# A two-block transformer on one core: attention and its projections in one stage

## The reference

```python
def diff_attention(q, k, v, q_gain, k_gain, ...):
    q = rms_norm(q, q_gain)
    k = rms_norm(k, k_gain)
    ...
    s = jnp.einsum('bqhmd,bkhmd->bhmqk', q_blk, k).astype(jnp.float32) * DIFF_HD ** -0.5
    s = jnp.where(dist >= 0, s + bias[None, :, None], NEG_INF)
    p = jax.nn.softmax(s, axis=-1)
    attn = (p[:, :, 0] - lam * p[:, :, 1]).astype(v.dtype)
```

## Time and profile before

| what | us |
|---|---|
| three runs | 3668.67, 3671.29 (median), 3679.3 |
| profiled execution, its own time | 3667.99 |
| its span | 3666.2 |
| differential projection and attention | about 252 to 418 |
| sliding-window projection and attention | about 440 to 567 |
| three dilated projections and attentions | about 2590 to 3015 |

### The profile page before, as it was taken

One profiled execution on the slowest core, in us unless ns is written; L12 is line 12 of the kernel. 1 busy time (PEld: TensorE's weight loads), 2 busy tenths in 40 slices (PEclk: granted clock), 3 DMA queues, 4 the chain that ended last, 5 costly groups with the idle time before them and its releaser, 6 DMA issues. The chain is left out here.

```text
span 3666.2 us, 46186 instructions
## 1 busy us (share of the span) xinstructions
PE 3096.4 (84%) x18486; PEld 2461.0 (67%) x18486; DVE 2236.7 (61%) x2018; ACT 1594.5 (43%) x1705; POOL 252.8 (7%) x149
## 2 busy tenths in 40 slices
PE   8747668995899999999999918788778777979999
PEld 6625446774688888887888716687546665767777
DVE  5246553343699989999999934465555454346543
ACT  5433232221577777777777704222233331233322
POOL 0000000002011111111111000242000000000000
PEclk9878679996799999999999958899879777989999
DMA  8211011221699999999999841000202111223322
GB/s 295 94 53 52 12 35 58 92 104 64 252 371 377 372 375 371 379 373 374 372 378 373 336 150 54 25 4 14 75 23 64 41 46 43 93 61 92 92 81 80
DMA packets 216481, 604.82 MB, mean 165 GB/s; under 512 B 11426, under 2 KB 108706, under 8 KB 182788
## 3 DMA queue, kind: packets, MB, share of 16 engines
q1 hardware_dynamic: 206960, 568.52, 42.6%
q0 software_dynamic: 9216, 33.56, 2.4%
q10 hardware_dynamic: 148, 0.53, 0.0%
HBM read 581.57 MB, written 21.01 MB: 164 GB/s over the span
## 5 line engine op out<-in xcount | busy, mean ns | idle before, releaser
L1661 DVE TENSOR_TENSOR weight_ring_part<-weight_ring,weight_ring_part 128x2048 fp32r<-128x2048 f32 x384 | 861.6, 2284 | 95.2 <-ACT weight_ring_part L1602 95.1
L1602 ACT ACTIVATE weight_ring_part<-weight_ring 128x2048 fp32r<-128x2048 f32 x384 | 721.2, 1915 | 249.2 <-PE ps L192 136.6
L192 PE MATMUL ps<-weight_ring_part 128*128 128x512 f32 (+1 forms) x1328 | 527.0, 397 | 0.0
L287 DVE TENSOR_TENSOR weight_ring_part<-weight_ring,weight_ring_part 128x2048 fp32r<-128x2048 f32 x135 | 308.1, 2283 | 353.7 <-ACT weight_ring_part L284 351.6
L284 ACT ACTIVATE weight_ring_part<-weight_ring 128x2048 fp32r<-128x2048 f32 x135 | 257.0, 1904 | 401.0 <-PE ps L192 178.5
L190 PE MATMUL ps<-weight_ring_part,gathered_hi 128*128 128x512 f32 x1024 | 409.6, 400 | 1.7 <-DVE gathered_lo L1670 1.7
L192 PE MATMUL ps<-weight_ring_part,gathered_hi 128*128 128x512 f32 x1024 | 406.0, 396 | 0.0
L191 PE MATMUL ps<-weight_ring_part,gathered_lo 128*128 128x512 f32 x1024 | 405.9, 396 | 0.0
L190 PE MATMUL ps<-h1T_hi,weight_ring_part 128*128 128x512 f32 (+1 forms) x776 | 317.7, 409 | 55.0 <-PEq L339 30.2
L191 PE MATMUL ps<-h1T_hi,weight_ring_part 128*128 128x512 f32 (+1 forms) x776 | 306.9, 395 | 0.0
L192 PEld LDWEIGHTS ps<-weight_ring_part 128*128 128x128 f32 (+1 forms) x1328 | 252.7, 190 | 57.2 <-issue 1.0
(11 more groups left out here) (451 smaller groups left out, 4881.9 us busy)
## 6 DMA issues: line engine op xcount, KB each, us to landing
weight_ring<-in_w SPq DMA_DIRECT2D x190, 2048.0 KB, 8.5
weight_ring<-in_w_in SPq DMA_DIRECT2D x58, 1024.0 KB, 5.3
weight_ring<-in_w_ada SPq DMA_DIRECT2D x24, 1024.0 KB, 5.2
weight_ring<-in_w_ffn_up SPq DMA_DIRECT2D x44, 512.0 KB, 5.0
weight_ring<-in_w_ffn_down SPq DMA_DIRECT2D x11, 1024.0 KB, 4.9
chosen_rows<-y_rows SPq DMA_DIRECT2D x4, 2048.0 KB, 13.4
weight_ring<-in_w_branch SPq DMA_DIRECT2D x6, 1024.0 KB, 5.0
x_tok<-in_x SPq DMA_DIRECT2D x2, 2048.0 KB, 9.3
```

The costliest lines, as they stand in the source:

```text
L192: return nc.tensor.matmul(out, x[0], y[1], start=False, stop=stop)
L287: self.nc.vector.tensor_tensor(lo, full, hi, ALU.subtract).then_inc(self.split, 1)
L1602: nc.scalar.activation(hi_half(h), full_half(h), ACT.Copy).then_inc(w_rounded, 1)
L1661: nc.vector.tensor_tensor(lo_half(h), full_half(h), hi_half(h), ALU.subtract).then_inc(w_split, 1)
```

## The change

The projection and the attention of each kind become one stage, streamed. All engines walk one list, plan, of products ("prod"), per-token sums ("sums"), key scalings ("spread") and attention beats ("beat"). plan_of makes it: the products of the first batch (v, then two chunks of q and two of k), then one product of the next batch, the sums, and the rest of the next batch's products with the batch's units laid between them. Batches of the differential attention have 8 and 8 units, those of the sliding window 4 and 4 (with all seven products ahead of them), those of the dilated groups 8, 8, 2, 2, 2, 2 in one stage of 36 products and 24 units. A unit of the last two groups is now one pair of heads with all four residues, not one residue with all heads. Products alternate between two banks, and v comes first.

The norms change: the squares of a 128-token tile are the stationary operand of a matmul with two columns of head_sum, so that a batch gets 32 sums a partition; root and reciprocal are taken on those. For q the factor is applied where the bias is added, one instruction per segment (head and map, or head and residue). For k it is written out to 512 columns, transposed by a matmul with the identity, and multiplied into the key tile; both gains and the scale go into the copy of k. The biases of the dilated groups are loaded by pairs of heads in the background.

```diff
@@ -348,11 +347,16 @@
...
-        for j in range(6):
-            ring.add_pair(wide(w_in, 512 * j), DK, 512, by_rows=(j == 4))
+        for j in range(2):
+            ring.add_pair(wide(w_in, 512 * j), DK, 512, by_rows=False)
+        ring.add_pair(wide(w_in, 2048), DK, 512, by_rows=True)
+        for half in range(2):
+            for j in (2, 3):
+                ring.add(wide(w_in, 512 * j)[:, :, 256 * half:256 * half + 256], DK, 256)
         w_kv = a["w_kv"].rearrange("(k p) n -> p k n", p=P)
         ring.add(w_kv[:, :, 0:256], DK, 256)
         ring.add(w_kv[:, :, 256:384], DK, P)
...
@@ -890,7 +897,350 @@
...
                             read_out(i - 3)
 
+        def plan_of(n_elements, batches, units_of, ahead=()):
+
+
+            plan, beat = [("prod", e) for e in range(batches[0]["ends"])], 0
+            for b, batch in enumerate(batches):
+                stop = batches[b + 1]["ends"] if b + 1 < len(batches) else n_elements
+                products = list(range(batch["ends"], stop))
+                beats = list(range(beat, beat + units_of[b]))
+                beat += units_of[b]
+                spreads = [("spread", (b, j)) for j in range(len(batch["keys"]))]
+                head, rest = products[:1], products[1:]
+                plan += [("prod", e) for e in head] + [("sums", b)]
+                slots = max(len(rest), 1)
+                for n in range(slots):
+                    if n < len(rest):
+                        plan.append(("prod", rest[n]))
+                    if n == 0:
+                        plan += spreads
+                    share = beats[len(beats) * n // slots:len(beats) * (n + 1) // slots]
+                    plan += [("beat", i) for i in share]
+            return plan + [("beat", beat + n) for n in range(3)]
...
+            def rounded_after(e):
+                x = elements[e]
+                if x["kind"] == "v" and not x["ends"]:
+                    return first_unit + x["unit"]
+                pair = e + 1 < len(elements) and x["ends"] and elements[e + 1]["kind"] == "v"
+                return first_unit + x["unit"] + (2 if pair else 1)
+
...
+                @block.tensor
+                def _(pe):
...
+                    def prod(e):
+                        x = elements[e]
+                        need = (0, 1) if x["kind"] == "v" else (0,)
+                        for u in (x["unit"] - (len(need) - 1) + n for n in need):
+                            if u not in w:
+                                w[u] = ring.take(pe)
+                        if e >= 2:
+                            copied(pe, e - 2)
...
+                        if x["ends"]:
+                            pe.wait_ge(group_ready, e + 1)
+                            for _ in range(x["ends"]):
+                                nc.tensor.nop().then_inc(ring.used, 1)
...
+                    def sums(b):
+                        pe.wait_ge(squared, squared_at[batches[b]["elements"][-1]])
...
+                        for j, e in enumerate(batches[b]["elements"]):
+                            for t in range(TT):
+                                at = 8 * j + 2 * t
+                                last = nc.tensor.matmul(ps[:, 2, at:at + 2], sq[:, slot_of_square(e), elements[e]["tokens"](t)], head_sum[:, 0:P:HD],
+                                                        start=True, stop=True)
+                        last.then_inc(summed, 1)
+
+                    def spread(b, j):
+                        pe.wait_ge(factors_ready, b + 1)
+                        pe.wait_ge(keys_scaled, spread_at[b, j])
+                        wide = sq[:, slot_of_square(batches[b]["keys"][j]), :]
+                        for t in range(TT):
+                            last = nc.tensor.matmul(ps[:, 2, P * t:P * t + P], wide[:, P * t:P * t + P], ident, start=True, stop=True)
+                        last.then_inc(spread_ready, 1)
...
+                    def beat(i):
+                        if 2 <= i < N + 2:
+                            u = units[i - 2]
+                            pe.wait_ge(probs_ready, i - 1)
+                            if i >= 3:
+                                pe.wait_ge(turned_read, i - 2)
+                            for j, c in enumerate(u["turns"]):
+                                last = nc.tensor.transpose(t_bank[:, P * j:P * j + P], s_buf[:, (i - 2) % 3, c:c + P], ident)
+                            last.then_inc(turned, 1)
...
+                            for c, n, lhsT, rhs, _, _ in u["scores"]:
+                                last = nc.tensor.matmul(scores[:, c:c + n], lhsT, rhs, start=True, stop=True)
+                            last.then_inc(scores_ready, 1)
...
+                @block.scalar
+                def _(act):
+                    def prod(e):
+                        x = elements[e]
+                        ring.ahead("act", act, first_unit + x["unit"])
+                        act.wait_ge(group_ready, e + 1)
...
+                        if x["kind"] == "k":
+                            nc.scalar.activation(x["dst"], ps[:, e % 2, :], ACT.Identity, scale=x["gain"], bias=0.0).then_inc(bank_free[e % 2], 1)
+                        else:
+                            nc.scalar.activation(x["dst"], ps[:, e % 2, :], ACT.Copy).then_inc(bank_free[e % 2], 1)
+                        ring.ahead("act", act, min(rounded_after(e), first_unit + n_units))
...
+                    def sums(b):
...
+                        nc.scalar.activation(root(b)[:, 0:m], ps[:, 2, 0:m], ACT.Sqrt, scale=1.0 / HD, bias=col("eps")).then_inc(rooted, 1)
...
+                @block.vector
+                def _(dve):
...
+                    def sums(b):
...
+                        nc.vector.reciprocal(factor(b)[:, 0:m], root(b)[:, 0:m])
+                        dve.drain()
+                        for e in batches[b]["keys"]:
+                            at = 8 * batches[b]["elements"].index(e)
+                            nc.vector.tensor_copy(sq[:, slot_of_square(e), :].rearrange("p (n d) -> p n d", n=8),
+                                                  factor(b)[:, at:at + 8].unsqueeze(2).to_broadcast([P, 8, HD]))
+                        dve.drain().then_inc(factors_ready, 1)
+
+                    def spread(b, j):
+                        e = batches[b]["keys"][j]
+                        copied(dve, e)
+                        dve.wait_ge(spread_ready, spread_at[b, j] + 1)
+                        dst = elements[e]["dst"]
+                        nc.vector.tensor_tensor(dst, dst, ps[:, 2, :], ALU.mult).then_inc(keys_scaled, 1)
...
+                            s_row = s_buf[:, i % 3, :]
+                            for c, m, _, _, q_at, bias in u["scores"]:
+                                last = nc.vector.scalar_tensor_tensor(s_row[:, c:c + m], scores[:, c:c + m], factor(u["batch"])[:, q_at:q_at + 1],
+                                                                      bias, ALU.mult, ALU.add)
+                            last.then_inc(scores_read, 1)
...
@@ -980,21 +1331,28 @@
-        project(hT, [[("norm", gains[:, 0:1], dqT[:, m, :], True) for m in range(BC)],
-                     [("norm", col("diff_knorm"), dkT[:, m, :], True) for m in range(BC)],
-                     token_groups(dv)], scratch4)
+        natural = lambda t: slice(P * t, P * t + P)
+        elements = [dict(kind="v", unit=1, ends=(2 if t == 3 else 0), dst=dv[:, t, :], tok=lambda h, k, t=t: h[:, k, P * t:P * t + P])
+                    for t in range(TT)]
+        for pair in range(2):
+            for kind, buf in (("q", dqT), ("k", dkT)):
+                for part in range(2):
+                    elements.append(dict(kind=kind, unit=2 + 2 * pair + (kind == "k"), part=part, ends=part, dst=buf[:, 2 * pair + part, :],
+                                         gain=gains[:, 0:1], tokens=natural))
+        batches = [dict(ends=8 + 4 * pair, elements=[4 + 4 * pair + n for n in range(4)], keys=[6 + 4 * pair, 7 + 4 * pair]) for pair in range(2)]
         units = []
...
-        attention(units, stats, s_buf, p_turned)
...
+        streamed(hT, elements, batches, units, plan_of(12, batches, [8, 8]), scratch4, factors, stats, s_buf, p_turned)
...
@@ -1028,36 +1386,31 @@
...
+        elements = [dict(kind="k", unit=0, part=g, ends=g, dst=skT[:, g, :], gain=gains[:, 1:2], tokens=natural) for g in range(2)]
+        elements.append(dict(kind="vT", unit=1, part=0, ends=1, dst=svT, turned=sv))
+        elements += [dict(kind="q", unit=2 + m // 2, part=m % 2, ends=m % 2, dst=sqT[:, m, :], tokens=natural) for m in range(BC)]
+        batches = [dict(ends=5, elements=[0, 1, 3, 4], keys=[0, 1], after_v=True), dict(ends=7, elements=[5, 6], keys=[], slot0=2)]
...
+        plan = plan_of(7, batches, [4, 4])
+        plan.insert(4, ("turn_v", 2))
+        streamed(hT, elements, batches, units, plan, scratch_x, factors, stats, s_buf, p_turned)
...
-            with stage("alibi_loaded") as (block, alibi_loaded):
...
```

(12 more changed lines are left out.)

382 lines of the change are left out of this document (295 added, 87 removed).

## The result

The changed kernel takes 3750.8 us (median of 4, 3750.6 to 3752.8) against 3673.5 for the kernel before in the same sessions: ratio 1.0209 (95% interval 1.0196 to 1.0223). Slower, as forecast, but by 77 us instead of the 30 of the forecast's sum, and above its range (3655 to 3722).

The account below looks back on a forecast made before the run. Projections were taken as bound by TensorE, attentions by the round of scores, softmax and transposes over three engines. Differential +28, sliding window +3 and dilated -1 make +30 on 3667.99, giving 3698 us; range 3655 to 3722.

Parts of the forecast that it names:

- the differential stage: Differential projection and attention streamed as one stage: +28 us, bounds +14 and +36.
- the open stretch ahead of unit 8: Differential attention: the second batch's chain of sums, root, reciprocal, copies and spreads stands open between units 7 and 8, 9 us.
- the sliding window: Sliding-window stage, all seven products ahead of unit 0, nothing overlapping: +3 us, bounds -4 to +9.
- rival A: Shared stages keep TensorE at 2.4 GHz, so units between products cost their floor: -12 us, 3656; chance 0.17.
- 415 to 435: Dilated stage: a length of 415 to 435 us in the profile after would show the forecast right.
- Three projections of 76.2 become 36 elements of 5.64 ... -25.5: Dilated stage: streamed products cost 67.7 us for twelve, without head sums and the waits following a product: -25.5 us.
- +14 for two waits and their cold starts: Dilated groups 1 and 2 begin with v again: wait 5.2 and cold start 1.8 us each, +14 us.
- +4.4 for other cold starts: Dilated stage: other cold starts of TensorE after tails, +4.4 us.
- Five more sums, 20.5, and spreads ... 22.8: Dilated stage: added per-token sums and six batches of key spreads at 3.3 to 5.4, +43.3 us, bounds 25 and 52.
- the sign of about 4 each: Profile after: each row of per-token sums takes about 4 us if the forecast is right.
- five of eight units lie between products and cost TensorE about 4.4: Last two dilated groups: units between products cost about 4.4 us each; attention units of the whole stage -24.4 us.
- Rival C: Queues of ScalarE and VectorE bind: +1.5 for each of 14 units between products, +21 us, 3719; chance 0.09 shared with another rival.

Follow-up runs that it names:

- Fillers: Changed kernel with 128-byte tile places plus eight filler matmuls of 128x512 a unit, results unread: 3733.5 us, against 3737.7 without them.
- runs of three: Changed kernel with 128-byte tile places, products behind each batch's first laid in runs of up to three instead of one by one: 3727.5 us against 3737.7.
- rearranged squares: Changed kernel with 128-byte tile places, query squares of groups 1 and 2 written in order of residues: 3723.5 us against 3737.7.
- earlier read-out: Changed kernel with 128-byte tile places, VectorE copying a unit's values out before waiting for the next weight unit's rounding: 3718.7 us against 3737.7.
- equal places: Both kernels with every tile of 2 KB a partition and more on multiples of 128 bytes: before 3674.8 us, changed 3737.7 us.

## Why the prediction was wrong

Right were the sign, the differential stage with its steps (waits of 4.81, sums 3.84, the open stretch ahead of unit 8 of 11.3 against 9, the start of scores within 1.2 us), the sliding window, and that rival A fails: the dilated stage's clock is 0.82 against 0.83. Table loads are 51 against 41, as forecast, at 1.28 us each, and where ScalarE had work ready it went on 0.01 us behind a load. In the dilated stage two of three groups begin with the 4.81 us wait (5.2 forecast); in group 1 units cover it. Three steps failed, all in that stage, which is 454 us long where 415 to 435 were to show the forecast right.

1. *"Three projections of 76.2 become 36 elements of 5.64 ... -25.5"*, with +14 for two waits and their cold starts and +4.4 for other cold starts. I priced a product in a shared stage as in a projection and let the clock fall in few places. These prices make 211 us for the 36 products; they took 232.1, 6.45 each, since 15 of them start low. With head sums and waits the term was -5.7 instead of -20.1 (14 us). Fillers take 13.4 off the products and runs of three take 8.6.

2. *"Five more sums, 20.5, and spreads ... 22.8"*. There are six sums, not five, and the price from the earlier trace rows holds only for tokens side by side at the high clock: in groups 1 and 2 a sum is 5.8 to 7.3 us, against the sign of about 4 each. Measured 32.5 + 23.2, 12 us above the term; shown by the rearranged squares (32.3 to 21.2). The spreads were right, and leaving them out is worth 44 us in the three attentions.

3. *"five of eight units lie between products and cost TensorE about 4.4"*: -24.4 for the units, measured -15.7 (9 us). I named the queue ("a copy and a split into VectorE's") and then priced it at half a microsecond; the copy of values behind the split costs up to 4.4 each, 21 us in seven places. Shown by the earlier read-out: 15.5 us in this stage.

These make the 35 us by which the dilated stage is off. Outside it I took untouched code to keep its time; it took 20 us more, from key_gain, 4 bytes wide: the idle tile alone gives 18 of them in the same stretches. With equal places the two kernels' untouched stages behind the first attentions agree, and the change alone costs 63 of the 77 us. The diff had a new tile in it, and I gave it no line in the sum.

Rival C had the right mechanism, queues of ScalarE and VectorE. That its +21 is the 21.2 us of waits is luck: it took 1.5 in each of 14 places, and there were seven of 3.0, where the copy of values stood behind the split. Its total, 3719, kept the forecast's price for the other two steps and had none for the tile.

That the overlap is not what costs is shown too: it is worth 22 to 29 us, and the rest of the change costs about 90. Priced one at a time in the version with overlap, the keys' factors are 40 to 44 of that and tokens four apart in the sums 11 to 14. How what is left divides (v first, the sums themselves, one instruction per segment) was not taken apart.

## What to carry to other kernels

Price a product that is laid between waits between its two clock levels, not by its row in a dense stretch (here 6.45 us instead of 5.64), and look in every engine's row at what stands behind an instruction that waits for another engine: the 0.28 us copy behind a split cost 21 us. Do not expect untouched code to keep its time when a change allocates a tile; compare the distance between matmuls in an untouched stage first. A new reduction by small matmuls should read its tokens side by side. Where a load looks slow, ask for its granted clock before its stride: both gave 330 ns here.

## What was not expected of the hardware

- The distance of two 128x512 matmuls goes by where their operand tiles lie: 227 ns where all are 128 bytes behind a multiple of 256, as the weight ring is, and 229 to 233 at the other places of the table. Whether 128 matters by itself or as the ring's own place was not tried; the ring was never moved.
- A 128x128 fp32 weight load takes 192 ns from columns side by side and 330 from columns four apart, both at a granted clock of 1.00; side by side at 0.50 it takes 333. In all four batches that load queries four apart the clock falls before the sum ends, in two for more than half of it; with all loads side by side it stays at 1.00 but for the last loads of a batch. Why it falls was not tried.
- Idle matmuls ahead of a wait paid in the kernel before (23 us, clock in the dilated stage 0.84 to 0.93) and hardly where products already stood between units (4 us, within the spread of the runs).
